# Latent attention: two heads at a time, with V as the weight and the division ahead of the transposes

## The chip, the cores and the metric

One Trainium2 chip, one of its cores. The kernel is one launch, and the metric is its device time in microseconds. Before the change three runs gave 4345.56, 4332.82 and 4324.17 us: a median of 4332.82.

## The reference, cut to what matters

The program computes two transformer blocks. The first has an RWKV mixer and then a latent attention (MLA), the second has two attentions with expert layers. The change lies in the latent attention: 16 heads, 512 queries, 768 keys (512 of the sequence and 256 of the context), 64 + 32 channels in a query or key, 64 in a value, all float32.

```python
def attend(q, k, v):
    s = jnp.einsum('bqhd,bkhd->bhqk', q, k) * (1.0 / math.sqrt(QK_NOPE + QK_ROPE))
    p = jax.nn.softmax(s, axis=-1)
    return jnp.einsum('bhqk,bkhd->bqhd', p, v)

    ...
    q = (rmsnorm(q_c, q_norm_g) @ w_qb)      # 16 heads of 64 + 32, the 32 rotated
    kv = (rmsnorm(kv_c, kv_norm_g) @ w_kvb)  # 16 heads of 64 + 64
    ...
    d_x = (o * jax.nn.silu(g_x)) @ w_out
```

## The kernel before, in words

The instructions of each engine are written out by hand, in program order, and held together by semaphores; nothing is scheduled by a tool. Data lie in one big arena (`K.arena`) and in the eight banks of PSUM (`K.ps`), 512 float32 columns each.

`MlaIn` projects the input and leaves the normed latents `QC` and `KC`, the rotated shared key `KPE` and the gate, already through silu, in `GATE` (channels on partitions). `MlaHeads` then works through 64 jobs, one for each head and block of 128 queries, four jobs of a head in a row. `Heads` holds what a job does:

- `pe_scores`: two products of 384 keys each into two banks, 0 and 1 or 2 and 3, with the query block as the weight (96x128).
- `dve_max`: VectorE takes the row maximum over 768 columns and scales it; `act_exp`: ScalarE writes the exponentials `P` and their sum.
- `pe_turn`: six 128x128 transposes of `P`, three into bank 4 and three into bank 5. VectorE copies bank 4 out (`dve_turned`, line 1550), ScalarE bank 5 (`act_turned`, line 1490), into `PT`.
- `pe_value`: six products with a piece of `PT` as the weight (128x128) and 64 columns of V, into bank 6. The queries lie on partitions there, so `dve_out` (line 1542) can divide by the sum as it copies out.

In round n TensorE issues the scores of job n, the value products of job n-2 and the transposes of job n-1:

```python
    def pe_round(self, pe, n):
        N = len(self.jobs)
        if 0 <= n < N:
            self.pe_scores(pe, n)
        if 0 <= n - 2 < N:
            self.pe_value(pe, n - 2)
        if 0 <= n - 1 < N:
            self.pe_turn(pe, n - 1)
```

Behind that each round has one piece of the projections of a head to come, given by `due(n)`: the query (3 products of 512 columns, weight 96 wide), the rope product (one), and the keys in two pieces (2 products of 384 columns each, weight 64 wide). All pieces use bank 7, so each waits until the last was copied out or used (`self.freed`). Head 0's four pieces come in rounds -5 to -2, head 1's query in round -1. V for heads 0 to 7 is made ahead of the rounds, V for heads 8 to 15 ahead of head 6's query, six groups of products one after the other, also in bank 7. POOL multiplies the query by the cosines and copies the shared key in; VectorE multiplies by the sines and adds.

`MlaOut` waits for all jobs, then transposes the output (queries on partitions) with 32 transposes into all eight banks (line 208), and VectorE gates them with eight products of 512 columns (line 1892). `FinalNorm.pe_context` comes next on TensorE: it waits for ScalarE's squares of the context (line 1927), which wait for the end of the jobs; then the output projection.

The second block's first attention, `AbHeads`, is not changed. It treats two heads at a time in the order that the change brings here: division at line 2353, copy of the turned banks at line 2321, value products at line 2283, copy of their result at line 2356.

Lines 202 and 208 are those of the helpers `mm` and `turn4`. A float32 product has two records in the trace.

Of the kernel before, what the change touches and what calls it, by code (L numbers as in the profile page):

```python
# [9 lines left out]
ALU = mybir.AluOpType  # L10
# [7 lines left out]
KT = 8  # L18
# [1387 lines left out]
class Heads:  # L1406

    def __init__(self, K, name, jobs, width, scale, value_banks):
        self.K, self.jobs, self.scale, self.value_banks = K, jobs, scale, value_banks
        s = K.s
        self.P = [K.take(T) for _ in range(4)]
        self.PT = [K.take(6, 128) for _ in range(2)]
        self.small = [K.take(8) for _ in range(12)]
        self.width = width
        self.scored, self.turned, self.valued = s[f"{name}_scored"], s[f"{name}_turned"], s[f"{name}_valued"]
        self.max, self.expd, self.sums, self.out = s[f"{name}_max"], s[f"{name}_exp"], s[f"{name}_sums"], s[f"{name}_out"]
        self.pt0, self.pt1 = s[f"{name}_pt0"], s[f"{name}_pt1"]  # L1420

        self.max_at, self.exp_at, self.sums_at = [0], [0], [0]
        for q, k, segs, masks, sink, v, kts, dst in jobs:
            copies = len(self.pieces(segs, masks)) if masks is not None else 0
            self.max_at.append(self.max_at[-1] + copies + (2 if sink is None else 3))
            self.exp_at.append(self.exp_at[-1] + (1 if sink is None else 2))
            self.sums_at.append(self.sums_at[-1] + (1 if sink is None else 2))

    @staticmethod
    def pieces(segs, masks):  # L1430

        found, o = [], 0
        for j, (a, w) in enumerate(segs):
            c = 0
            while c < w:
                d = 128
                mk = masks.get((j, c))
                while mk is None and c + d < w and (j, c + d) not in masks:
                    d += 128
                found.append((j, c, o, d, mk))  # L1440
                o += d
                c += d
        return found

    def view(self, n):

        _, _, segs, masks, _, _, _, _ = self.jobs[n]
        P, nk = self.P[n % 4], sum(w for _, w in segs)
        if masks is not None:
            return P[:, 0:nk], P[:, 0:nk], nk  # L1450
        w = segs[0][1]
        sl = 2 * (n % 2)
        return self.K.ps[:, sl:sl + len(segs), 0:w], P[:, 0:nk].rearrange("p (s n) -> p s n", n=w), nk

    def halves(self, n):
        nt = sum(w for _, w in self.jobs[n][2]) // 128
        return (0, (nt + 1) // 2), ((nt + 1) // 2, nt)

    def pe_scores(self, pe, n):
        q, k, segs, _, _, _, _, _ = self.jobs[n]  # L1460
        if n >= 2:
            pe.wait_ge(self.expd, self.exp_at[n - 1])
        for j, (a, w) in enumerate(segs):
            ins = mm(pe, self.K.ps[:, 2 * (n % 2) + j, 0:w], [(q, k[:, a:a + w])])
        ins.then_inc(self.scored, 1)

    def pe_turn(self, pe, n):
        K, P = self.K, self.P[n % 4]
        pe.wait_ge(self.expd, self.exp_at[n + 1])
        for h, (c0, c1) in enumerate(self.halves(n)):  # L1470
            if n:
                pe.wait_ge((self.pt0, self.pt1)[h], n)
            turn4(pe, K.ps[:, 4 + h, :], [P[:, c * 128:(c + 1) * 128] for c in range(c0, c1)], K.C("ident")).then_inc(self.turned, 1)

    def pe_value(self, pe, n):
        _, _, _, _, _, v, kts, dst = self.jobs[n]
        nb = len(self.value_banks)
        pe.wait_ge(self.pt0, n + 1)
        pe.wait_ge(self.pt1, n + 1)
        if n >= nb:  # L1480
            pe.wait_ge(self.out, n - nb + 1)
        mm(pe, self.K.ps[:, self.value_banks[n % nb], 0:self.width], [(self.PT[n % 2][:, c, :], v[:, kt, :]) for c, kt in enumerate(kts)]
           ).then_inc(self.valued, 1)

    def act_turned(self, act, n):
        c0, c1 = self.halves(n)[1]
        act.wait_ge(self.turned, 2 * n + 2)
        if n >= 2:
            act.wait_ge(self.valued, n - 1)
        act.activation(self.PT[n % 2][:, c0:c1, :], self.K.ps[:, 5, 0:(c1 - c0) * 128].rearrange("p (c t) -> p c t", t=128), ACT.Copy  # L1490
                       ).then_inc(self.pt1, 1)

    def act_exp(self, act, n):
        _, _, _, _, sink, _, _, _ = self.jobs[n]
        src, dst, _ = self.view(n)
        sm = self.small[n % 12]
        act.wait_ge(self.max, self.max_at[n + 1])
        if n >= 4:
            act.wait_ge(self.turned, 2 * (n - 4) + 2)
        act.activation(dst, src, ACT.Exp, bias=sm[:, 0:1], scale=self.scale, accum_out=sm[:, 1:2]).then_inc(self.expd, 1)  # L1500
        if sink is not None:
            act.activation(sm[:, 2:3], sm[:, 0:1], ACT.Exp, bias=sink).then_inc(self.expd, 1)

    def dve_max(self, dve, n):
        _, _, segs, masks, sink, _, _, _ = self.jobs[n]
        src, _, _ = self.view(n)
        mx, at = self.small[n % 12][:, 0:1], self.max_at[n]
        dve.wait_ge(self.scored, n + 1)
        if masks is not None:
            if n >= 4:  # L1510
                dve.wait_ge(self.turned, 2 * (n - 4) + 2)
            for j, c, o, d, mk in self.pieces(segs, masks):
                ps, at = self.K.ps[:, 2 * (n % 2) + j, c:c + d], at + 1
                if mk is None:
                    dve.tensor_copy(src[:, o:o + d], ps).then_inc(self.max, 1)
                else:
                    dve.tensor_tensor(src[:, o:o + d], ps, mk, ALU.add).then_inc(self.max, 1)
            dve.wait_ge(self.max, at)
        if n >= 12:
            dve.wait_ge(self.sums, self.sums_at[n - 11])  # L1520
        dve.tensor_reduce(mx, src, AX.XY if masks is None else AX.X, ALU.max).then_inc(self.max, 1)  # L1521
        dve.wait_ge(self.max, at + 1)
        if sink is None:
            dve.tensor_scalar(mx, mx, -self.scale, None, ALU.mult).then_inc(self.max, 1)
        else:
            dve.tensor_scalar(mx, mx, self.scale, sink, ALU.mult, ALU.max).then_inc(self.max, 1)
            dve.wait_ge(self.max, at + 2)
            dve.tensor_scalar(mx, mx, -1.0, None, ALU.mult).then_inc(self.max, 1)

    def dve_sums(self, dve, n):  # L1530
        sink, sm = self.jobs[n][4], self.small[n % 12]
        dve.wait_ge(self.expd, self.exp_at[n + 1])
        if sink is not None:
            dve.tensor_tensor(sm[:, 1:2], sm[:, 1:2], sm[:, 2:3], ALU.add).then_inc(self.sums, 1)
            dve.wait_ge(self.sums, self.sums_at[n] + 1)
        dve.reciprocal(sm[:, 1:2], sm[:, 1:2]).then_inc(self.sums, 1)

    def dve_out(self, dve, n):
        nb = len(self.value_banks)
        dve.wait_ge(self.valued, n + 1)  # L1540
        dve.wait_ge(self.sums, self.sums_at[n + 1])
        dve.tensor_scalar(self.jobs[n][7], self.K.ps[:, self.value_banks[n % nb], 0:self.width], self.small[n % 12][:, 1:2], None, ALU.mult
                          ).then_inc(self.out, 1)

    def dve_turned(self, dve, n):
        c0, c1 = self.halves(n)[0]
        dve.wait_ge(self.turned, 2 * n + 1)
        if n >= 2:
            dve.wait_ge(self.valued, n - 1)
        dve.tensor_copy(self.PT[n % 2][:, c0:c1, :], self.K.ps[:, 4, 0:(c1 - c0) * 128].rearrange("p (c t) -> p c t", t=128)  # L1550
                        ).then_inc(self.pt0, 1)

    def pe_round(self, pe, n):
        N = len(self.jobs)
        if 0 <= n < N:
            self.pe_scores(pe, n)
        if 0 <= n - 2 < N:
            self.pe_value(pe, n - 2)  # L1560
        if 0 <= n - 1 < N:
            self.pe_turn(pe, n - 1)

    def act_round(self, act, n):
        N = len(self.jobs)
        if 0 <= n - 1 < N:
            self.act_turned(act, n - 1)
        if 0 <= n < N:
            self.act_exp(act, n)

    def dve_round(self, dve, n):
        N = len(self.jobs)
        if 0 <= n < N:
            self.dve_max(dve, n)
# [1993 lines left out]
```

## Time and profile before

| what | us |
|---|---|
| median of three runs | 4332.82 |
| the profiled execution, its own time | 4321.39 |
| its span, first to last instruction | 4319.3 |
| latent attention, first score product to last | 316.6 |
| from there to the end of the last job | 7.5 |
| output transposes and gating, to the next product | 5.7 |

The profile is of one execution. "PE" is TensorE's products, "PEld" its weight loads, which run ahead of and beside the products; DVE is VectorE, ACT ScalarE, POOL GpSimd. An idle time is put down to the engine and line that ended it. Ends of products are modelled, and starts of loads are not.

### The profile page before, as it was taken

The page shows a single profiled execution, that of the slowest core. Times are in us where ns is not written, and L with a number is a line of the kernel's source. Part 1 is how long each engine was busy: PE and PEld are TensorE (multiplying, and loading weights), DVE is VectorE, ACT ScalarE, POOL GpSimd, SP SyncE. Part 2 cuts the span into 40 slices and gives each one's busy share as a digit, 9 for nine tenths or more (in the row PEclk, how much of TensorE's full clock was granted, in tenths as well). Part 3 has the DMA queues.
Part 4 walks back from the last instruction along what each step waited for, and adds up shares of the span by engine and source line. Part 5 has one row for each costly group of instructions (what it writes and reads, how often), then busy time and mean ns, then how long its engine had stood idle before and what let it go on. Part 6 is the DMA issues. An engine that isn't in the chain of part 4 may idle for free. (4 is left out here: it accounts for less than half of the span.)

```text
span 4319.3 us, 76089 instructions
## 1 busy us (share of the span) xinstructions
PE 3788.0 (88%) x32246; PEld 2141.1 (50%) x32246; DVE 1546.7 (36%) x3763; ACT 1353.7 (31%) x2940; POOL 197.2 (5%) x193
## 2 busy tenths in 40 slices
PE   7998687877777999998988979999969988799997
PEld 4554566666664546664565533333345454333332
DVE  3011666666673104442247231111132183211112
ACT  2002334433433123332546222222235262222222
POOL 0000000000000001000100000000012000000000
PEclk9998899999998999999999989999979999899998
DMA  5223344444443200001210249999833102699996
GB/s 207 76 84 122 93 126 120 120 115 124 118 135 99 102 22 1 20 20 38 60 46 1 101 147 386 390 390 392 329 136 92 46 1 106 252 389 386 390 394 269
DMA packets 314587, 696.04 MB, mean 161 GB/s; under 512 B 169216, under 2 KB 195968, under 8 KB 289152
## 3 DMA queue, kind: packets, MB, share of 16 engines
q1 hardware_dynamic: 293024, 612.41, 39.7%
q0 software_dynamic: 14048, 53.49, 3.6%
q10 hardware_dynamic: 7168, 25.17, 1.5%
q8 instruction: 260, 4.26, 0.4%
q14 instruction: 87, 0.71, 0.1%
HBM read 624.94 MB, written 63.71 MB: 159 GB/s over the span
## 5 line engine op out<-in xcount | busy, mean ns | idle before, releaser
L202 PE MATMUL ps<-arena 128*128 128x512 f32 (+7 forms) x5388 | 1547.7, 452 | 90.8 <-ACT arena L1137 23.9
L202 PEld LDWEIGHTS ps<-arena 128*128 128x128 f32 (+3 forms) x5388 | 889.4, 192 | 716.8 <-issue 455.8
L2693 PE MATMUL ps<-arena 128*32 128x512 f32 x9216 | 1025.7, 598 | 29.2 <-DMA arena<-in_w 24.6
L2693 PEld LDWEIGHTS ps<-arena 128*32 128x32 f32 x9216 | 307.0, 110 | 649.9 <-issue 632.9
L620 PE MATMUL ps<-arena 64*64 64x64 f32 (+1 forms) x10624 | 458.3, 240 | 176.2 <-DVE arena L1194 65.7
L620 PEld LDWEIGHTS ps<-arena 64*64 64x64 f32 x10624 | 409.5, 145 | 256.0 <-issue 105.4
L2827 DVE COPY arena<-ps 128x384 f32<-128x384 f32 x64 | 35.7, 558 | 657.1 <-PE ps L2752 657.1
L208 PE MATMUL ps<-arena 128*128 128x128 f32 x1200 | 189.9, 293 | 81.3 <-DVE arena L3146 38.0
L2803 ACT ACTIVATE arena<-ps 96x512 f32<-96x512 f32 x64 | 38.0, 593 | 624.2 <-PE ps L2693 624.2
L208 PEld LDWEIGHTS ps<-arena 128*128 128x128 f32 x1200 | 144.3, 153 | 122.7 <-DVE arena L3146 41.1
L600 DVE SCALAR_TENSOR_TENSOR arena<-arena 128x769 f32<-128x769 f32 x48 | 45.7, 1016 | 276.2 <-PE ps L202 275.9
L400 DVE SCALAR_TENSOR_TENSOR arena<-ps,arena 128x512 f32<-128x512 f32 (+1 forms) x48 | 31.8, 662 | 285.9 <-PE ps L202 285.9
L2845 DVE TENSOR_TENSOR arena<-ps,arena 64x512 f32<-64x512 f32 x64 | 43.7, 682 | 226.5 <-ACT arena L2815 226.5
L552 ACT ACTIVATE arena<-ps 128x512 f32<-128x512 f32 x64 | 30.9, 490 | 280.5 <-PE ps L202 261.5
L1521 DVE TENSOR_REDUCE arena<-ps 128x1 f32<-128x768 f32 x64 | 61.3, 958 | 158.3 <-PE ps L202 158.3
L962 PE MATMUL ps<-arena 64*64 64x64 f32 x2304 | 100.3, 243 | 16.5 <-DVE arena L1276 12.7
L2815 ACT ACTIVATE arena<-ps 64x512 f32<-64x512 f32 x64 | 38.0, 593 | 244.7 <-PE ps L2693 244.7
L344 PE MATMUL ps<-arena 128*128 128x512 f32 (+1 forms) x208 | 86.5, 581 | 20.4 <-ACT arena L335 20.4
L962 PEld LDWEIGHTS ps<-arena 64*64 64x64 f32 x2304 | 87.9, 155 | 26.7 <-DVE arena L1276 18.3
L2858 POOL DMA_INDIRECT arena<-htok,arena x64 | 57.8, 903 | 948.2 <-PE ps L2752 937.7
L253 ACT ACTIVATE arena<-arena 128x768 f32<-128x768 f32 (+1 forms) x32 | 24.5, 786 | 233.6 <-DVE arena L400 233.6
L2618 DVE TENSOR_REDUCE arena<-ps 128x1 f32<-128x768 f32 x64 | 61.0, 953 | 87.1 <-PE ps L202 87.1
(281 smaller groups left out, 3672.6 us busy)
## 6 DMA issues: line engine op xcount, KB each, us to landing
arena<-in_w SPq DMA_DIRECT2D x192, 2048.0 KB, 30.1
arena<-in_w_mod SPq DMA_DIRECT2D x24, 2048.0 KB, 8.8
arena<-in_mod_w SPq DMA_DIRECT2D x12, 2048.0 KB, 9.0
yb<-arena ACTq DMA_DIRECT2D x64, 384.0 KB, 10.0
arena<-in_rwkv_w_in SPq DMA_DIRECT2D x8, 2048.0 KB, 9.9
arena<-rkvg SPq DMA_DIRECT2D x38, 384.0 KB, 4.0
rkvg<-arena POOLq DMA_DIRECT2D x32, 384.0 KB, 3.0
arena<-di SPq DMA_DIRECT2D x192, 64.0 KB, 2.5
```

The costliest lines, as they stand in the source:

```text
L202: ins = pe.matmul(out, l, r, start=(i == 0), stop=(i == len(pairs) - 1))
L208: ins = pe.transpose(bank[:, i * 128:(i + 1) * 128], src, ident)
L344: ins = pe.matmul(out, w[:, k, :], self.H[:, k, a:a + n], start=(k == 0), stop=(k == KT - 1), skip_group_check=True)
L600: dve.scalar_tensor_tensor(self.LPs[j % 2][:, k, 1:n + 1], self.XX[:, k, 1:n + 1], self.K.PR("mu")[:, 8 * j + k:8 * j + k + 1], self.H[:, ...
L620: ins = pe.matmul(out[p, :], l[p, :], r[p, :], start=(i == 0), stop=(i == len(pairs) - 1))
L962: ins = pe.matmul(out[p, :], src[p, :], ident[p, p], start=True, stop=True)
L1521: dve.tensor_reduce(mx, src, AX.XY if masks is None else AX.X, ALU.max).then_inc(self.max, 1)
L2618: dve.tensor_reduce(sm[:, c:c + 1], self.scores_at(n, c), AX.XY, ALU.max).then_inc(self.max, 1)
L2693: return pe.matmul(bank[32 * at:32 * at + 32, :], left[:, k, 32 * g:32 * g + 32], right[:, k, :], start=first, stop=last)
L2803: act.activation(self.moe.AC[i % 2][0:ROWS, :], A[0:ROWS, :], ACT.Silu).then_inc(self.silu, 1)
L2845: dve.tensor_tensor(YS[0:64, 512:1024], ps[0:64, 7, :], YS[0:64, 512:1024], ALU.add).then_inc(self.y1, 1)
L2858: pool.indirect_dma_start(out=moe.HG[i % 3][0:ROWS, :], out_offset=None, in_=self.K.scr["htok"][0:moe.nt, :], in_offset=bass.IndirectOffse ...
```

## The change

Jobs are taken for two heads at a time: jobs 8i to 8i+7 alternate between heads 2i and 2i+1. Q, K and their pieces have four buffers each in place of two, and both heads of a pair must be ready before its first job, so pieces start at round -9. VectorE takes the reciprocal of the sum and multiplies `P` by it ahead of the transposes, which come three jobs late; one ScalarE copy empties both banks. The value products of two jobs come together in odd rounds, with V as the weight (64 wide), one head into partitions 0 to 63 of bank 6 and the other into 64 to 127. Channels lie on partitions then, so the copy out of the bank also gates, and `MlaOut`'s transposes and gating go.

```diff
-class Heads:
...
 class MlaHeads:
...
+    FIRST, LAST = -9, 68
...
-        self.VV, self.OT = K.take(6, D), K.take(4, D)
-        self.Qs, self.Ks = [K.take(TX) for _ in range(2)], [K.take(T) for _ in range(2)]
+        self.VV, self.O = K.take(6, D), K.take(KT, TX)
+        self.Qs, self.Ks = [K.take(TX) for _ in range(4)], [K.take(T) for _ in range(4)]
...
-        h, part = divmod(n + 5, 4)
+        h, part = divmod(n + 9, 4)
         return (h, part) if 0 <= h < 16 else None
+    @staticmethod
+    def job(n):
+        return 2 * (n // 8) + n % 2, n % 8 // 2
...
+    def pe_turn(self, pe, n):
+        pe.wait_ge(self.normed, n + 1)
+        if n:
+            pe.wait_ge(self.pt, n)
+        for b in range(2):
+            ins = turn4(pe, self.K.ps[:, 4 + b, :], [self.P[n % 4][:, i * 128:(i + 1) * 128] for i in range(3 * b, 3 * b + 3)], self.K.C("ident"))
+        ins.then_inc(self.turned, 1)
+
+    def pe_value(self, pe, p):
+        pe.wait_ge(self.pt, 2 * p + 2)
+        if p:
+            pe.wait_ge(self.out, p)
+        for t in range(6):
+            for c in range(2):
+                h, _ = self.job(2 * p + c)
+                ins = pe.matmul(self.K.ps[64 * c:64 * c + 64, 6, 0:128], self.VV[:, t, 64 * h:64 * h + 64], self.PT[c][:, t, :], start=(t == 0),
+                                stop=(t == 5), skip_group_check=True)
+        ins.then_inc(self.valued, 1)
...
-        for n in range(-5, 66):
...
-            self.heads.pe_round(pe, n)
+        for n in range(self.FIRST, self.LAST):
+            if 0 <= n < self.N:
+                if n % 8 == 0:
+                    h = n // 4 + 1
...
+                self.pe_scores(pe, n)
+            if n >= 5 and n % 2:
+                self.pe_value(pe, (n - 5) // 2)
+            if 0 <= n - 3 < self.N:
+                self.pe_turn(pe, n - 3)
             if due := self.due(n):
...
+            j = n - 3
+            if 0 <= j < self.N:
+                act.wait_ge(self.turned, j + 1)
+                if j >= 2:
+                    act.wait_ge(self.valued, j // 2)
+                act.activation(self.PT[j % 2].rearrange("p (b i) t -> p b (i t)", b=2), ps[:, 4:6, 0:384], ACT.Copy).then_inc(self.pt, 1)
+            if 0 <= n < self.N:
+                sm = self.small[n % 8]
+                act.wait_ge(self.max, 2 * n + 2)
...
+                act.activation(self.P[n % 4].rearrange("p (s n) -> p s n", s=2), self.scores(n), ACT.Exp, bias=sm[:, 0:1], scale=self.SCALE,
+                               accum_out=sm[:, 1:2]).then_inc(self.expd, 1)
...
+            j = n - 1
+            if 0 <= j < self.N:
+                sm, P = self.small[j % 8], self.P[j % 4]
+                dve.wait_ge(self.expd, j + 1)
+                dve.reciprocal(sm[:, 2:3], sm[:, 1:2]).then_inc(self.sums, 1)
+                dve.wait_ge(self.sums, j + 1)
+                dve.tensor_scalar(P, P, sm[:, 2:3], None, ALU.mult).then_inc(self.normed, 1)
+            if n >= 5 and n % 2:
+                p = (n - 5) // 2
+                h, qb = self.job(2 * p)
+                at = self.O[:, h // 2, 128 * qb:128 * qb + 128]
+                dve.wait_ge(self.valued, p + 1)
+                dve.tensor_tensor(at, ps[:, 6, 0:128], self.into.GATE[:, h // 2, 128 * qb:128 * qb + 128], ALU.mult).then_inc(self.out, 1)
...
 class MlaOut:
...
         self.heads.over(pe)
-        for i in range(8):
-            qb, c = divmod(i, 2)
-            turn4(pe, K.ps[:, i, :], [self.heads.OT[:, qb, m * 128:(m + 1) * 128] for m in range(4 * c, 4 * c + 4)], K.C("ident")
-                  ).then_inc(s["mla_chan"], 1)
-        pe.wait_ge(s["mla_gated"], 8)
         fin.pe_context(pe)
         self.proj.pe(pe, fin)
```

How it moves TensorE's instructions. In the steady loop, from one head's query piece on, before (L202 128x64 x6 are the value products, 128x384 x2 the scores, 64x384 x2 a key piece, 96x512 x3 the query, 96x512 the rope product, L208 the transposes):

```order
L202 MATMUL ps<-arena 96x512 x3
L202 MATMUL ps<-arena 128x384 x2
L202 MATMUL ps<-arena 128x64 x6
L208 MATMUL ps<-arena 128x128 x6
L202 MATMUL ps<-arena 96x512
L202 MATMUL ps<-arena 128x384 x2
L202 MATMUL ps<-arena 128x64 x6
L208 MATMUL ps<-arena 128x128 x6
L202 MATMUL ps<-arena 64x384 x2
```

and with the change (L1633 are the new value products):

```order
L202 MATMUL ps<-arena 96x512 x3
L202 MATMUL ps<-arena 128x384 x2
L208 MATMUL ps<-arena 128x128 x6
L202 MATMUL ps<-arena 96x512
L202 MATMUL ps<-arena 128x384 x2
L1633 MATMUL ps<-arena 64x128 x12
L208 MATMUL ps<-arena 128x128 x6
L202 MATMUL ps<-arena 64x384 x2
```

Every second round has no value products, and the others have twelve, of 128 columns.

At the end of the stage, before:

```order
L208 MATMUL ps<-arena 128x128 x6
L202 MATMUL ps<-arena 128x64 x6
L208 MATMUL ps<-arena 128x128 x6
L202 MATMUL ps<-arena 128x64 x6
L208 MATMUL ps<-arena 128x128 x32
L202 MATMUL ps<-arena 128x256 x8
```

and with the change, from the last scores on:

```order
L202 MATMUL ps<-arena 128x384 x2
L1633 MATMUL ps<-arena 64x128 x12
L208 MATMUL ps<-arena 128x128 x12
L1633 MATMUL ps<-arena 64x128 x12
L208 MATMUL ps<-arena 128x128 x12
L1633 MATMUL ps<-arena 64x128 x12
L202 MATMUL ps<-arena 128x256 x8
```

The 32 transposes are gone, and four turns and three pairs of value products now follow the last scores, where two turns and three jobs' value products did.

VectorE in one round with a rope product, before:

```order
L1521 TENSOR_REDUCE arena<-ps 128x1
L1524 TENSOR_SCALAR arena<-arena 128x1
L1536 RECIPROCAL arena<-arena 128x1
L1542 TENSOR_SCALAR arena<-ps,arena 128x64
L1550 COPY arena<-ps 128x384
L1842 TENSOR_TENSOR arena<-ps,arena 96x512
```

and with the change:

```order
L1724 TENSOR_REDUCE arena<-ps 128x1
L1726 TENSOR_SCALAR arena<-arena 128x1
L1731 RECIPROCAL arena<-arena 128x1
L1733 TENSOR_SCALAR arena<-arena 128x768
L1747 TENSOR_TENSOR arena<-ps,arena 96x512
```

The division over 768 columns takes the place of the copy of 384 and of the division on the way out; the gated copy (line 1739) stands in odd rounds only.

## Rows read from the trace of the kernel before

**Rows 1.** The page, part 1: busy us, share of the span, instructions.
```profile
PE 3788.0 (88%) x32246; PEld 2141.1 (50%) x32246; DVE 1546.7 (36%) x3763; ACT 1353.7 (31%) x2940; POOL 197.2 (5%) x193
```
**Rows 2.** Windows: the loop and the drain; us, busy by engine, clock, DMA.
```profile
1632.90:1949.50 316.60, 312.37 (x1620) 206.51 (x1619) 145.18 (x341) 113.93 (x239) 31.23 (x30) 1.00 0.04 14
1949.50:1957.00 7.50, 5.92 (x49) 5.26 (x47) 3.31 (x9) 2.24 (x6) 0.00 (x0) 1.00 0.01 3
```
**Rows 3.** Waits in 1632.9 to 1949.5: total us, times, longest.
```profile
ACT arena L1490 <- PE ps L208: 170.4, 62, 3.0
DVE arena L1521 <- PE ps L202: 157.3, 63, 19.6
```
**Rows 4.** Timeline, weight loads, rounds without a piece: start us, us, what.
```profile
1941.06 0.70 PEld L208 LDWEIGHTS ps<-arena 128*128 128x128 f32 x6
1941.72 2.71 PEld L202 LDWEIGHTS ps<-arena 96*128 96x128 f32 x16
1944.30 0.69 PEld L208 LDWEIGHTS ps<-arena 128*128 128x128 f32 x6
```
**Rows 5.** Timeline, weight loads: value products of the last job but one, alone.
```profile
1952.31 1.42 PEld L202 LDWEIGHTS ps<-arena 128*128 128x128 f32 x12 [0.83 <-DVE arena L1550]
1953.59 0.70 PEld L208 LDWEIGHTS ps<-arena 128*128 128x128 f32 x6
```
**Rows 6.** Timeline, transposes' loads over one head's four rounds.
```profile
1747.10 0.70 PEld L208 LDWEIGHTS ps<-arena 128*128 128x128 f32 x6
1751.19 0.70 PEld L208 LDWEIGHTS ps<-arena 128*128 128x128 f32 x6
...
1766.75 0.70 PEld L208 LDWEIGHTS ps<-arena 128*128 128x128 f32 x6
```
**Rows 7.** Timeline of the second block's first attention.
```profile
2350.41 0.64 PEld L208 LDWEIGHTS ps<-arena 128*128 128x128 f32 x6 [0.17 <-issue]
2351.33 0.81 ACT L2321 ACTIVATE arena<-ps 128x768 f32<-128x768 f32 x1 [0.55 <-PE ps L208]
2352.25 0.64 PEld L208 LDWEIGHTS ps<-arena 128*128 128x128 f32 x6 [0.73 <-DVE arena L2353]
2353.05 1.29 PEld L2283 LDWEIGHTS ps<-arena 128*64 128x64 f32 x24 [0.17 <-issue]
...
2354.51 0.64 PEld L208 LDWEIGHTS ps<-arena 128*128 128x128 f32 x6 [0.17 <-issue]
```
**Rows 8.** Timeline, TensorE: head 0's query piece, and head 1's, its first.
```profile
1621.03 2.79 PE L202 MATMUL ps<-arena 128*96 128x512 f32 x6 [0.78 <-ACT arena L1810]
...
1630.62 6.26 PE L202 MATMUL ps<-arena 128*96 128x512 f32 x16 [0.57 <-ACT arena L1830]
```
**Rows 9.** Groups in 2217 to 2415: busy us, mean ns, idle before.
```profile
L2336 DVE TENSOR_REDUCE arena<-ps 128x1 f32<-128x768 f32 x32 | 30.5, 953 | 12.0 <-PE ps L2253 12.0
L2353 DVE TENSOR_SCALAR arena<-arena 128x768 f32<-128x768 f32 x32 | 18.4, 618 | 0.6
L2356 DVE COPY arena<-ps 128x128 f32<-128x128 f32 x47 | 13.5, 287 | 30.4 <-PE ps L2283 29.9
...
L2321 ACT ACTIVATE arena<-ps 128x768 f32<-128x768 f32 x47 | 38.1, 811 | 29.5 <-PE ps L208 29.5
L2311 ACT ACTIVATE arena<-ps,arena 128x768 f32<-128x768 f32 x32 | 28.7, 900 | 3.7 <-DVE arena L2339 3.1
L2311 ACT ACTIVATION_READ_ACCUMULATOR arena<-ps,arena 128x1 f32 x88 | 17.7, 201 | 0.0
```
**Rows 10.** Timeline: the last job's copy, the context's squares, the context's product.
```profile
1956.71 0.28 DVE L1542 TENSOR_SCALAR arena<-ps,arena 128x64 f32<-128x64 f32 x1 [1.92 <-PE ps L202]
1957.03 1.91 ACT L1927 ACTIVATE arena<-arena 128x2048 f32<-128x2048 f32 x1 [1.98 <-DVE arena L1542]
...
1962.68 0.70 PE L202 MATMUL ps<-arena 128*128 128x256 f32 x2 [1.91 <-DVE arena L1892]
```
**Rows 11.** Waits in 2217 to 2415: total us, times, longest.
```profile
PEld ps L208 <- DVE arena L2353: 22.4, 25, 1.3
```

More of the change, by code:

```diff
@@ L1405, in over @@
         e.wait_ge(self.proj.added, self.proj.total)
-class Heads:
[L1411 to L1574, printed above, removed]
-        if 0 <= n - 1 < N:
-            self.dve_sums(dve, n - 1)
-        if 0 <= n - 2 < N:
-            self.dve_out(dve, n - 2)
-        if 0 <= n - 1 < N:
-            self.dve_turned(dve, n - 1)
-    def over(self, e):
-        N = len(self.jobs)
-        e.wait_ge(self.out, N)
-        e.wait_ge(self.pt1, N)
-        e.wait_ge(self.sums, self.sums_at[N])
@@ L1599, in __init__ @@
         self.sq, self.rk, self.kw = K.take(5, T), K.take(T), K.take(SLOT)
+        self.end = K.top
         self.sums = Sums(K, "mlan", [self.sq[:, k, :] for k in range(2)], self.rstd, T)
@@ L1732, in __init__ @@
         K.top = into.inner
-        self.VV, self.OT = K.take(6, D), K.take(4, D)
-        self.Qs, self.Ks = [K.take(TX) for _ in range(2)], [K.take(T) for _ in range(2)]
+        self.VV, self.O = K.take(6, D), K.take(KT, TX)
+        self.Qs, self.Ks = [K.take(TX) for _ in range(4)], [K.take(T) for _ in range(4)]
         self.rt = K.take(TX)
-        jobs = []
-        for h in range(16):
-            for qb in range(4):
-                jobs.append((self.Qs[h % 2][0:96, qb * 128:(qb + 1) * 128], self.Ks[h % 2][0:96, :], SEGS, None, None,
-                             self.VV[:, :, 64 * h:64 * h + 64], range(6), self.OT[:, qb, 64 * h:64 * h + 64]))
-        self.heads = Heads(K, "mla", jobs, 64, 1.0 / math.sqrt(96), (6,))
+        self.P = [K.take(T) for _ in range(4)]
+        K.top = max(K.top, into.end)
+        self.PT = [K.take(6, 128) for _ in range(2)]
+        self.small = [K.take(4) for _ in range(8)]
         s = K.s
         self.mm, self.evac = s["mlah_mm"], s["mlah_evac"]
-        self.O = None
+        self.scored, self.turned, self.valued = s["mlah_scored"], s["mlah_turned"], s["mlah_valued"]
+        self.max, self.expd, self.sums, self.normed = s["mlah_max"], s["mlah_exp"], s["mlah_sums"], s["mlah_normed"]
+        self.pt, self.out = s["mlah_pt"], s["mlah_out"]
     def mm_at(self, h, what):
@@ L1755, in due, with scores @@
     def due(n):
-        h, part = divmod(n + 5, 4)
+        h, part = divmod(n + 9, 4)
         return (h, part) if 0 <= h < 16 else None
+    @staticmethod
+    def job(n):
+        return 2 * (n // 8) + n % 2, n % 8 // 2
+    def scores(self, n):
+        return self.K.ps[:, 2 * (n % 2):2 * (n % 2) + 2, 0:384]
     def over(self, e):
-        self.heads.over(e)
+        e.wait_ge(self.out, self.N // 2)
     def pe_values(self, pe, c):
@@ L1834, in dve @@
         self.into.over(dve)
-        for n in range(-5, 66):
-            self.heads.dve_round(dve, n)
+        for n in range(self.FIRST, self.LAST):
+            if 0 <= n < self.N:
+                mx = self.small[n % 8][:, 0:1]
+                dve.wait_ge(self.scored, n + 1)
+                if n >= 8:
+                    dve.wait_ge(self.normed, n - 7)
+                dve.tensor_reduce(mx, self.scores(n), AX.XY, ALU.max).then_inc(self.max, 1)
+                dve.wait_ge(self.max, 2 * n + 1)
+                dve.tensor_scalar(mx, mx, -self.SCALE, None, ALU.mult).then_inc(self.max, 1)
+            j = n - 1
[11 more added lines that the diff above has]
+                dve.tensor_tensor(at, ps[:, 6, 0:128], self.into.GATE[:, h // 2, 128 * qb:128 * qb + 128], ALU.mult).then_inc(self.out, 1)
             if due := self.due(n):
                 h, part = due
-                Q = self.Qs[h % 2][0:96, :]
+                Q = self.Qs[h % 4][0:96, :]
                 if part == 1:
                     dve.wait_ge(self.mm, self.mm_at(h, "rope"))
+                    if h:
+                        dve.wait_ge(s["mlah_rope"], 2 * h)
                     dve.tensor_tensor(self.rt[0:96, :], ps[0:96, 7, :], K.C("mS")[0:96, 0:TX], ALU.mult).then_inc(s["mlah_rope"], 1)
@@ L1867, in __init__ @@
         self.K, self.s, self.into, self.heads = K, K.s, into, heads
-        self.O = K.take(KT, TX)
-        self.proj = OutProj(K, "mla", K.I["mla_w_out"], [self.O[:, k, :] for k in range(KT)], K.MODS[1], 16, ((0, 0, TX),),
+        self.proj = OutProj(K, "mla", K.I["mla_w_out"], [heads.O[:, k, :] for k in range(KT)], K.MODS[1], 16, ((0, 0, TX),),
                             ((heads.mm, heads.mm_at(7, "q")), (heads.mm, heads.mm_at(15, "q"))), first=3)
```

46 lines of the change are left out of this document (23 added, 23 removed).

## The prediction, made before the changed kernel was run

> **What bounds the kernel now.** I read the page first: on one core TensorE is busy for 88% of the span [rows 1], more than twice any other engine. The change touches one stage only, the latent attention, so everything after is read there. The windows [rows 2] show it from the first score matmul at 1632.9 us to the last at 1949.5: 316.6 us, TensorE busy 312.4, VectorE 145.2, ScalarE 113.9, and the granted clock 1.00, the full 2.4 GHz. The waits [rows 3] say who waits: ScalarE (170.4 us before its copies) and VectorE (157.3 us before its maxima) both wait for TensorE. So the loop is worth what its TensorE instructions issue, and I price it from the starts of weight loads, which unlike modelled matmul ends are events: a group costs the time to the next group's first load.
>
> **TensorE's round today.** Without a projection piece one round (six transposes, two scores, six value products) takes 1944.30 - 1941.06 = 3.24 us, of which the transposes take 1941.72 - 1941.06 = 0.66 [rows 4]. Six value products alone take 1953.59 - 1952.31 = 1.28 [rows 5]. That leaves 1.30 for the scores. A head's four rounds take 1766.75 - 1747.10 = 19.65 us [rows 6], so the four projection pieces issue for 19.65 - 4 x 3.24 = 6.69 us a head; the rope piece alone for 1751.19 - 1747.10 - 3.24 = 0.85.
>
> **1. The value products.** Each job's six products with a 128x128 weight (the turned exponentials) and 64 columns become, for two jobs, twelve with a 128x64 weight (V) and 128 columns, alternately into the lower and the upper half of the bank. This form runs already in the next attention, at line 2283: 24 records (two to a float32 product) take 2354.51 - 2353.05 = 1.46 us, with 0.17 us of nothing behind the last load, and the transposes ahead of them take 0.80 in place of 0.66 [rows 7]. I take a pair at 1.46 + 0.80 - 0.66 = 1.60 us against 2 x 1.28 = 2.56 now: 0.96 saved, times 32 pairs: **-30.7 us**. The bounds: 24 records at half of a 64-column product's issue (1.28/12/2 = 0.053 us) without any gap give 1.28 and -41.0; the two halves not overlapping give 24 x 0.107 + 0.31 = 2.9 and +11. I take the row of the same shape, the nearest there is. By the first sentence alone the term would be the -41.0; the gaps in rows 7 agree with the second, and this kernel pays them twice a pair.
>
> **2. Two heads before the first score.** The rounds now begin at -9 and not -5: head 1's four pieces run bare behind head 0's, where before three lay in rounds 0 to 2. Bare, each waits for the copy of the one before, since all share bank 7: head 0 took 1630.62 - 1621.03 = 9.6 us [rows 8] for 6.7 of issue. **+2.9 us**.
>
> **3. The loop's other waits.** Transposes come three jobs late, so a job's chain (maximum, exponential, division) has two more rounds. Only one pair of banks receives transposes, as before, but now one ScalarE copy of 768 columns empties both (0.81 us) in place of a 384 copy on each of two engines. From a turn's first load through its copy to the next dependent load takes 2352.25 - 2350.41 = 1.84 us [rows 7], so 1.18 us after the turn's issue is over. Between a turn and the next product or turn that needs its copy TensorE has the next scores, 1.30, and the piece: 1.30 + 0.85 = 2.15 or more while pieces last. It fits everywhere, by 0.1 us where there are none. ScalarE's exponential (0.90 and an accumulator read of 0.20) stands behind the copy in its queue. In the last nine rounds, which have no piece (before it was five), an odd job's exponential ends some 0.15 us after the scores that reuse its banks could start: four times, **+0.6 us**. VectorE has per job 0.95 for the maximum, 0.62 for the division over 768 columns and 0.29/2 for the gated copy (priced as the copy of line 2356), 1.7 us, and its one-column instructions and rope work as now; ScalarE 0.81 + 0.90 + 0.20 = 1.9 us and its copies of pieces as now [rows 9]. TensorE's mean round becomes (19.65 - 2 x 0.96)/4 = 4.43. So the division and the larger copy I cost at nothing: TensorE's issue hides them. If that cover went, they would cost 0.62 + 0.81 us a job, 92 us. The V set for heads 8 to 15 moves four rounds ahead and costs what it did. POOL's two instructions a head run a full round before they are needed. SP's second load of output weights starts four rounds sooner and was not waited for.
>
> **4. The drain.** After the last scores TensorE still issues four turns and three value pairs, 4 x 0.66 + 3 x 1.60 = 7.4 us, with four waits of 1.18 us for a copy (turn 61, pair 60-61, turn 63, pair 62-63) and some 0.6 us to the end of the last gated copy: 12.7. Before it was the 7.5 us window [rows 2], for 2 x 0.66 + 3 x 1.28 = 5.2 us of issue. The extra idle time is (12.7 - 7.4) - (7.5 - 5.2) = **+3.0 us**.
>
> **5. The end.** The 32 transposes of the output and the eight gating products go. From the end of the last copy, 1956.71 + 0.28, to the next product at 1962.68 was 5.7 us [rows 10]. The next product is the context's sum, which needs ScalarE's squares: 1.91 us, started when heads are over, hidden so far under the gating. It is late next: 1.91 + 0.15 stay. **-3.6 us**.
>
> **Sum.** -30.7 + 2.9 + 0.6 + 3.0 - 3.6 = -27.8 us. Against the profiled execution's own 4321.4 us: 4293.6. That execution lies 11.4 us below the median of the three runs, 4332.8; set against the median, as the result will be, it is **4305 us**, 0.64% less. Nothing downstream has a fixed date: the loads of the next part start on semaphores of this one and move with it.
>
> **Rivals.** *The pair does not overlap* (here V, not turned exponentials, is the weight for both, and the two moving operands differ): 2.9 us a pair, so +11 in place of -30.7, and with the other terms +14 us: 4347, within 0.5%. Rows 7 speak against it: there, too, the two halves have different moving operands. Chance 0.04.
>
> *TensorE waits at every turn* (the slower side). This order of work, run in the next attention, does leave TensorE waiting: 22.4 us in 25 waits for the division at line 2353 [rows 11]. The place is the turn: it waits for the job's division and for the copy of the turn before. If each of 64 turns waited a further 1 us, +64 gives +36 us: 4369. Today's time is crossed at 27.8/64 = 0.43 us a turn, and ahead of that the margins must go: 0.1 us in rounds without a piece, 2.15 - 1.18 = 1.0 with the shortest piece. Against it: there the rounds have no projection pieces to fill the time, here 55 of 64 have. A rule of the Trainium skill feeds this one (SBUF — State Buffer, its part on the port pair that VectorE and GpSimd share): a VectorE tensor_scalar over SBUF can hold or wait for that pair for a whole instruction. By it a division could stand behind one of POOL's two instructions a head; no row here has both at once. Chance 0.07.
>
> *The gain is mostly eaten by small stalls*: 0.2 us a round, as where a queue's order bites, gives 13 us back: -15, 4318, within 0.5%. For it: margins of 0.1 us in the tail, and two more switches of tile shape beside scores than rows 7 can show. Chance 0.19.
>
> *The change does nothing at all* cannot be: the order of instructions shows the twelves and no 32 transposes.
>
> **How the numbers follow.** The forecast (-28, give or take 6) has 0.70. About 0.5%, 21.7 us, is what a measurement of this kernel can tell from no change; the forecast lies just past it, so a tenth of its chance falls short of that by the scatter of a median (the three runs span 21 us), and a little comes back from the small-stall case. Faster 0.66, within 0.5% 0.27, slower 0.07. Range: down to the gap-free pair and scatter, -41 + 3 - 9, 4286; up to the small-stall case with scatter of 8, 4326. What is left out is the slower case, the part without overlap, and bad luck.
>
> **What would show it.** Right: 24 records of the new value line in about 1.3 us of loads; even rounds with rope of 2.8 us and a cycle of four rounds of 17.7; head 1 bare before the first score, which comes 9.6 us later after the first projection; 12.7 us from last score to last gated copy; then 2.1 to the context's product; clock 1.00. Wrong: TensorE waiting for the division or the copy inside the loop for over 10 us in all, a pair of more than 2 us, or a granted clock under 1.00 in the stage.

## The result, and the profile after

The changed kernel took 4304.05 us, the median of five runs (4298.65 to 4305.8), against 4332.82 us, the median of five runs of the kernel before (4324.17 to 4345.56): a ratio of 0.9935, 95% interval 0.9921 to 0.9948. The forecast was 4305 us.

TensorE's share on the page is nearly what it was in [rows 1], with 29 us less of busy time:

```profile
PE 3759.1 (87%) x32214; PEld 2095.4 (49%) x32214; DVE 1533.8 (36%) x3723; ACT 1372.6 (32%) x2940; POOL 201.0 (5%) x193
```

The profiled execution's span is 4300.9 us, only 18.4 less than before, though the medians differ by 28.8. The stage has to be looked at by itself. These are TensorE's rows from its first V group on (start us, us, what, idle time before and what ended it), in the trace of the kernel before and then of the changed one:

```profile
1604.83 1.98 PE L202 MATMUL ps<-arena 128*128 128x512 f32 x4 [0.69 <-ACT arena L1685]
```

```profile
1613.91 1.98 PE L202 MATMUL ps<-arena 128*128 128x512 f32 x4 [0.69 <-ACT arena L1505]
...
1630.11 2.79 PE L202 MATMUL ps<-arena 128*96 128x512 f32 x6 [0.78 <-ACT arena L1681]
...
1639.71 2.81 PE L202 MATMUL ps<-arena 128*96 128x512 f32 x6 [0.57 <-ACT arena L1713]
...
1649.25 12.10 PE L202 MATMUL ps<-arena 128*96 128x512 f32 x32 [0.57 <-ACT arena L1713]
...
1943.68 11.85 PE L202 MATMUL ps<-arena 128*128 128x256 f32 x35 [2.42 <-ACT arena L1818]
```

The stage began 9.1 us later in this execution, ahead of anything that the change touches. From the first V group to the context's product it took 1962.68 - 1604.83 = 357.85 us before and 1943.68 - 1613.91 = 329.77 us now: **-28.1 us**. I call this the stage's time below; it moves far less between executions than the span does. From that product to the end it was 2356.6 us before and 2357.2 now.

The loop, TensorE's weight loads over four rounds, which answer to [rows 6]:

```profile
1677.37 1.29 PEld L1633 LDWEIGHTS ps<-arena 128*64 128x64 f32 x24 [0.55 <-issue]
1678.83 0.64 PEld L208 LDWEIGHTS ps<-arena 128*128 128x128 f32 x6 [0.17 <-issue]
...
1695.08 1.29 PEld L1633 LDWEIGHTS ps<-arena 128*64 128x64 f32 x24 [0.55 <-issue]
1696.54 0.64 PEld L208 LDWEIGHTS ps<-arena 128*128 128x128 f32 x6 [0.17 <-issue]
```

Four rounds take 1696.54 - 1678.83 = 17.71 us in place of 19.65: 0.97 us less for each pair. The new value products issue for 1.46 us, as they do in [rows 7].

The drain, in which TensorE, VectorE and ScalarE take turns:

```profile
1928.28 1.53 PE L1633 MATMUL ps<-arena 128*64 128x128 f32 x24
1929.74 0.87 PE L208 MATMUL ps<-arena 128*128 128x128 f32 x6
1931.61 0.85 PE L208 MATMUL ps<-arena 128*128 128x128 f32 x6 [0.99 <-ACT arena L1693]
1933.35 1.53 PE L1633 MATMUL ps<-arena 128*64 128x128 f32 x24 [0.90 <-ACT arena L1693]
1934.82 0.87 PE L208 MATMUL ps<-arena 128*128 128x128 f32 x6
1936.68 0.85 PE L208 MATMUL ps<-arena 128*128 128x128 f32 x6 [0.99 <-ACT arena L1693]
1938.43 2.83 PE L1633 MATMUL ps<-arena 128*64 128x128 f32 x24 [0.90 <-ACT arena L1693]
```

```profile
1941.30 0.29 DVE L1739 TENSOR_TENSOR arena<-ps,arena 128x128 f32<-128x128 f32 x1 [6.08 <-PE ps L1633]
```

```profile
1941.62 1.91 ACT L1818 ACTIVATE arena<-arena 128x2048 f32<-128x2048 f32 x1 [3.25 <-DVE arena L1739]
```

All four waits for ScalarE's copy (line 1693) are there, and the last pair takes 2.83 us and not 1.53. The windows answer to [rows 2] and tell why. The third last number of a row is the granted clock, as a fraction of 2.4 GHz:

```profile
1651.40:1928.10 276.70, 272.58 (x1556) 155.82 (x1554) 135.16 (x307) 127.38 (x234) 31.37 (x28) 1.00 0.05 16
1928.10:1938.40 10.30, 6.54 (x73) 5.13 (x72) 3.18 (x9) 4.72 (x8) 0.00 (x0) 1.00 0.00 0
1938.40:1941.50 3.10, 2.83 (x24) 2.43 (x24) 0.20 (x1) 0.00 (x0) 0.00 (x0) 0.51 0.00 0
...
1943.60:1948.00 4.40, 4.32 (x18) 3.53 (x19) 0.00 (x0) 0.00 (x0) 0.00 (x0) 1.00 0.02 4
```

The last pair ran at 0.51, about 1.2 GHz, behind a drain with four waits. Before, a stretch of low clock came one step later, behind the gating, on the context's product:

```profile
1962.60:1967.00 4.40, 4.32 (x12) 3.53 (x13) 0.02 (x1) 0.00 (x0) 0.00 (x0) 0.61 0.00 0
```

### The profile page after: what moved, and what is told of

The parts are those of the page before. It is cut to its first block and busy times, and to the rows that moved or that the text cites. A ratio compares the mean times of both kernels' runs of the same rounds, so it can differ in the third digit from the quotient of the medians.

```text
span 4300.9 us, 75825 instructions
## 1 busy us (share of the span) xinstructions
PE 3759.1 (87%) x32214; PEld 2095.4 (49%) x32214; DVE 1533.8 (36%) x3723; ACT 1372.6 (32%) x2940; POOL 201.0 (5%) x193
## 5 line engine op out<-in xcount | busy, mean ns | idle before, releaser
L202 PE MATMUL ps<-arena 128*128 128x512 f32 (+8 forms) x4620 | 1458.6, 479 | 95.6 <-ACT arena L1137 23.9
L202 PEld LDWEIGHTS ps<-arena 128*128 128x128 f32 (+5 forms) x4620 | 786.5, 190 | 707.1 <-issue 457.4
L2584 PE MATMUL ps<-arena 128*32 128x512 f32 x9216 | 1022.6, 596 | 31.1 <-DMA arena<-in_w 26.5
L620 PEld LDWEIGHTS ps<-arena 64*64 64x64 f32 x10624 | 415.3, 146 | 255.2 <-issue 103.5
L208 PE MATMUL ps<-arena 128*128 128x128 f32 x1168 | 189.0, 296 | 83.6 <-DVE arena L3037 41.4
L208 PEld LDWEIGHTS ps<-arena 128*128 128x128 f32 x1168 | 140.3, 150 | 140.2 <-DVE arena L3037 44.9
L1724 DVE TENSOR_REDUCE arena<-ps 128x1 f32<-128x768 f32 x64 | 61.3, 958 | 142.3 <-PE ps L202 142.3
L962 PEld LDWEIGHTS ps<-arena 64*64 64x64 f32 x2304 | 92.0, 161 | 25.8 <-DVE arena L1276 17.8
L216 PE MATMUL ps<-arena 128*32 128x512 f32 x576 | 75.5, 646 | 19.6 <-DMA arena<-in_w_mod 15.5
```

Of the source, the lines that this page charges most:

```text
L202: ins = pe.matmul(out, l, r, start=(i == 0), stop=(i == len(pairs) - 1))
L208: ins = pe.transpose(bank[:, i * 128:(i + 1) * 128], src, ident)
L216: ins = pe.matmul(out[32 * j:32 * j + 32, :], cs[:, 4 * half + j, :], w[:, 4 * half + j, :], start=(half == 0), stop=(half == 1))
L620: ins = pe.matmul(out[p, :], l[p, :], r[p, :], start=(i == 0), stop=(i == len(pairs) - 1))
L962: ins = pe.matmul(out[p, :], src[p, :], ident[p, p], start=True, stop=True)
L1724: dve.tensor_reduce(mx, self.scores(n), AX.XY, ALU.max).then_inc(self.max, 1)
```

## The experiments

All are variants of the changed kernel; all times are medians, and "the stage's time" is from the profiled execution, first V group to the context's product. Each variant was profiled once, and the changed kernel was not run beside the later ones, so they are compared with it by the stage's time. That time needs one correction. Three microseconds or so of low clock fall on the last pair in the changed kernel, inside the stage; in other variants they fall on the context's product, just behind it, or do not come. These are the last pair and that product with the halves apart, with two jobs late, and with more banks:

```profile
1971.87 2.46 PE L1633 MATMUL ps<-arena 128*64 128x128 f32 x24 [0.90 <-ACT arena L1693]
1976.74 19.11 PE L202 MATMUL ps<-arena 128*128 128x256 f32 x48 [2.41 <-ACT arena L1818]
```

```profile
1933.13 1.53 PE L1633 MATMUL ps<-arena 128*64 128x128 f32 x24 [0.90 <-ACT arena L1693]
1937.08 19.11 PE L202 MATMUL ps<-arena 128*128 128x256 f32 x48 [2.43 <-ACT arena L1818]
```

```profile
1913.20 1.53 PE L1642 MATMUL ps<-arena 128*64 128x128 f32 x24 [0.90 <-ACT arena L1706]
1917.15 17.43 PE L202 MATMUL ps<-arena 128*128 128x256 f32 x48 [2.43 <-ACT arena L1831]
```

In the changed kernel the same two took 2.83 and 17.43; with the halves apart 2.46 is what every pair takes. A pair at full clock is worth 1.3 us of the stage's time; the product at low clock costs 1.7 us behind the stage, where that time does not see it.

The changed kernel run again beside the first three variants:

> The changed kernel again, as the yardstick on this chip for the runs beside it: 28 us under the kernel before, 0.6 to 0.7%.

It took 4304.97 us against 4332.79 for the kernel before: ratio 0.994, interval 0.9924 to 0.9957. The stage's time was 329.76 us, within 0.01 of the other execution's, although the stage began at 1609.23 and not at 1613.91 us.

**Are the two halves worth it, or the narrow weight?**

```diff
-        for t in range(6):
-            for c in range(2):
+        for c in range(2):
+            for t in range(6):
                 h, _ = self.job(2 * p + c)
```

> The same twelve value products of a pair, but all six of one head first, then all six of the other, so that neighbours go to the same half of the columns. Theory (the two halves run side by side, and that is the gain): a pair costs 24 records at 0.107 us and 0.3 for the switches, 2.9 us in place of 1.6; 32 pairs give +41 us over the changed kernel, some 13 us over the kernel before. Rival (the gain is the narrow weight, or the moving of 128 columns per load): the pair stays at 1.6 us and the time that of the changed kernel.

4335.19 us, ratio 1.000 (0.9989 to 1.0011) to the kernel before, 30.2 us over the changed one run beside it; stage's time 358.02, 28.3 more. The value products' loads and what follows them:

```profile
1683.11 2.21 PEld L1633 LDWEIGHTS ps<-arena 128*64 128x64 f32 x24 [0.55 <-issue]
1685.49 0.64 PEld L208 LDWEIGHTS ps<-arena 128*128 128x128 f32 x6 [0.17 <-issue]
```

A pair issues for 1685.49 - 1683.11 = 2.38 us and not 1.46: 0.92 us for each of 32 pairs is 29.4 us. The stage shows 28.3 because its last pair ran at full clock, 1.3 us less; with the 1.7 us behind the stage it comes to 30.0, against 30.2 by the medians. So the gain of the change hangs on the alternation between the two halves; V as a narrow weight without it keeps 0.04 of the 0.96 us a pair. The rival is refuted. My price for this case was too high all the same: a record takes 2.38/24 = 0.099 us, gaps included, not the 0.107 that I had taken from products with a weight 128 wide.

**Is the division hidden?** A second instruction behind it:

```diff
-                dve.tensor_scalar(P, P, sm[:, 2:3], None, ALU.mult).then_inc(self.normed, 1)
+                dve.tensor_scalar(P, P, sm[:, 2:3], None, ALU.mult).then_inc(s["mlah_extra"], 1)
+                dve.wait_ge(s["mlah_extra"], j + 1)
+                dve.tensor_scalar(P, P, 1.0, None, ALU.mult).then_inc(self.normed, 1)
```

> A second VectorE instruction over the 768 exponentials (times 1.0) behind the division, 64 times 0.62 us = 40 us of added VectorE work ahead of the transposes. Theory (VectorE is hidden with two rounds to spare): +0 to 2 us over the changed kernel, all of it in the last nine rounds, and TensorE waits for the division in less than 2 us. Rival (the chain through the division is exposed in part): +10 to +40 us.

4306.13 us, 1.2 over the changed kernel; stage's time 329.74, the same to 0.02 us, with 48.2 us more of work on VectorE. The groups (busy us, mean ns, idle before):

```profile
L1724 DVE TENSOR_REDUCE arena<-ps 128x1 f32<-128x768 f32 x64 | 61.0, 953 | 95.1 <-PE ps L202 95.1
L1735 DVE TENSOR_SCALAR arena<-arena 128x768 f32<-128x768 f32 x64 | 48.2, 753 | 2.2
```

VectorE's wait for scores shrank from 142.3 to 95.1 us, by the work that was added: it is cover, and the division, itself 39.7 us of VectorE's work, costs no time that the stage shows. To see where the cover ends, three added instructions:

> Three further VectorE instructions over the 768 exponentials behind the division. The second cost VectorE 0.75 us a job and the clock nothing; three cost 2.3 us a job, so VectorE has 1.7 + 0.3 + 0.3 + 2.3 = 4.7 us of work a job against 4.4 us that TensorE issues. Theory (the cover is TensorE's issue, and it ends there): VectorE becomes the bound, +0.3 us for each of 55 jobs with a piece and 4.3 - 2.8 = 1.5 us for the nine without, some +30 us over the changed kernel. Rival (the chain of one job counts, not the sum: two rounds of 4.4 us hide 2.3 us more): +0 to 5 us in the rounds with pieces, under +15 in all.

4323.48 us against 4327.41 for the kernel before beside it, ratio 0.9995 (0.9984 to 1.0006): some 24 us over the changed kernel by the ratios, stage's time 349.29, 19.5 more. That is between the theory (30) and its rival (under 15). Two of TensorE's rows show what neither had:

```profile
1904.74 2.99 PE L202 MATMUL ps<-arena 128*64 128x384 f32 x8 [0.72 <-DVE arena L1753]
...
1922.07 1.56 PE L202 MATMUL ps<-arena 96*128 96x384 f32 x4 [0.94 <-ACT arena L1699]
```

With pieces, TensorE waits not for the division but for VectorE's rope product, which is queued behind it and holds bank 7: 9.8 us in 13 waits up to 1905 us. From 1655 to 1905 us VectorE was busy for 212 of 250 us, some 4.2 us for each of 51 jobs and not 4.7, so it was not the bound there. In rounds without pieces it nearly was (39 of the next 41 us): the exponentials come late, because VectorE's maxima do, and the waits from there to the end of the drain make most of the other half of the 19.5 us. The context's product took 20.37 us, 2.9 more than in the changed kernel, at low clock, which takes the 19.5 to 22.4 of the 24. The cover is 0.75 us a job at least and less than 2.3.

**Do the transposes have to be three jobs late?** Two variants move them, and the value products with them (here for one job late):

```diff
-            if n >= 5 and n % 2:
-                self.pe_value(pe, (n - 5) // 2)
-            if 0 <= n - 3 < self.N:
-                self.pe_turn(pe, n - 3)
+            if n >= 3 and n % 2 == 1:
+                self.pe_value(pe, (n - 3) // 2)
+            if 0 <= n - 1 < self.N:
+                self.pe_turn(pe, n - 1)
```

> Transposes one job late and not three, value products one round behind. Theory: the division of job n-1 stands on VectorE behind the maximum of job n, which waits for its scores, so it ends 2.3 us after them; TensorE waits that long in rounds without value products and 0.7 us in the others: 3.0 us a pair, 96 us in all, less 2 us in the drain: some +94 us over the changed kernel, and the wait named is that for the division's line. Rival (lateness is not needed, the copy decides): under +10 us.

4432.22 us, 127.3 over the changed kernel, ratio 1.0229 (1.0207 to 1.025) to the kernel before; stage's time 453.99, 124.2 more. The waits of the loads and of the products (total us, times, longest) and two of the transposes' loads:

```profile
PEld ps L208 <- DVE arena L1733: 104.7, 62, 2.6
PE ps L208 <- DVE arena L1733: 77.8, 62, 2.0
```

```profile
1802.23 0.64 PEld L208 LDWEIGHTS ps<-arena 128*128 128x128 f32 x6 [2.58 <-DVE arena L1733]
...
1808.92 0.64 PEld L208 LDWEIGHTS ps<-arena 128*128 128x128 f32 x6 [0.74 <-DVE arena L1733]
```

The mechanism is as forecast, long waits where there are no value products and short ones where there are. The size is not, and the windows say why. The clock was granted at 0.90 over these 405 us; the second and third rows are the whole stage, first V group to the context's product, one job late and in the changed kernel:

```profile
1655.00:2060.00 405.00, 323.06 (x1593) 172.68 (x1592) 136.66 (x308) 129.87 (x236) 29.16 (x28) 0.90 0.03 11
1618.42:2072.41 453.99, 356.47 (x1712) 186.00 (x1713) 142.58 (x320) 141.58 (x254) 34.37 (x32) 0.91 0.03 10
1609.23:1938.99 329.76, 309.82 (x1712) 172.53 (x1713) 141.37 (x320) 140.56 (x254) 36.58 (x32) 0.99 0.04 14
```

TensorE's same 1712 records were busy for 46.7 us more and TensorE was idle for 77.6 us more, 124.2 in all. So the waits came to less than the forecast's 94 us, and the rest is slower products. The clock gives that rest its size: a tenth below full speed on average is a fifth of the time, 81 us, at 1.2 GHz, and if TensorE was busy through all of it that costs 40 us. What is left is near the error of the split, since ends of products are modelled and one that a wait follows counts as busy to its end. I read it that waits of this length cost a second time, through the clock; no run holds the clock and keeps the waits, so that the waits bring the clock down is not shown.

> Transposes two jobs late, value products in even rounds. Theory (two is enough: the division ends 2.3 us after the next scores, and TensorE needs it 2.8 us or more after them; the drain is one round shorter): -1 us against the changed kernel, no wait for the division in the loop. Rival (three are needed): waits for the division of about 0.5 us a round, +30 us.

4300.04 us, ratio 0.9939 (0.9919 to 0.996) to the kernel before, which took 4331.42 in this set of runs; stage's time 327.20, 2.6 less than the changed kernel's. No wait for the division is listed in the loop. So two jobs late is enough, and the rival is refuted. Of the 2.6 us, 1.3 is the last pair at full clock, and it is no gain: the low clock moved to the context's product and cost 1.7 us there. The other 1.3 is the drain that is a round shorter. With both moves of the clock 0.9 us is left, the forecast's 1, and too little for the medians to tell.

**What the bare stretches cost.** Both sets of V and the pieces of heads 0 and 1 spread over the free banks:

```diff
+    @staticmethod
+    def piece_bank(h, part):
+        return 7 - part if h < 2 else 7
...
-            pe.wait_ge(*self.freed)
-            mm(pe, self.K.ps[:, 7, :], [(self.into.KC[:, k, tt * 128:(tt + 1) * 128], kw[:, k, 8 * c:8 * c + 8, 64:128]) for k in range(2)]
+            b = 7 - tt if c == 0 else 7 - tt % 2
+            if c == 1 and tt == 1:
+                self.freed[b] = self.out, self.v_after
+            pe.wait_ge(*self.freed[b])
+            mm(pe, self.K.ps[:, b, :], [(self.into.KC[:, k, tt * 128:(tt + 1) * 128], kw[:, k, 8 * c:8 * c + 8, 64:128]) for k in range(2)]
...
```

> The changed kernel with both sets of V and the pieces of heads 0 and 1 spread over several banks in place of bank 7 alone, so that only the rope product waits for a copy. Theory (these stretches pay a bare copy per group): 10 gaps of 0.95 us between the V groups, 0.9 twice behind them, and 2.0 us for each of two heads: -15 us against the changed kernel, half before the first scores. Rival (the copies on ScalarE set the pace, or the gaps hide nothing): under 4 us.

4282.63 us, ratio 0.9891 (0.9874 to 0.9907); stage's time 312.27, 17.5 less than the changed kernel's. TensorE ahead of the first scores:

```profile
1604.88 13.14 PE L202 MATMUL ps<-arena 128*128 128x512 f32 x30 [0.69 <-ACT arena L1505]
1618.70 6.57 PE L202 MATMUL ps<-arena 96*96 96x512 f32 x16 [0.68 <-ACT arena L1722]
1625.95 15.85 PE L202 MATMUL ps<-arena 96*96 96x512 f32 x42 [0.68 <-ACT arena L1722]
```

Three waits are left, two of them for the query's own copy. From the first V group to the first transposes it takes 36.8 us in place of 47.3, 10.5 less, of which 4.7 lie from head 0's rope product on, in the pieces of heads 0 and 1; that is more than the 2.9 us of waiting that the change had added there. The second V set, 1714.96 to 1734.83 up to the next transposes in the changed kernel, takes 5.7 us less. Together these are 16.2 us for the 15 forecast; the other 1.3 of the 17.5 is the last pair at full clock.

**What the context's product waits for.** The squares also move in the arena, to where the weights of keys and values were, since their own place overlaps buffers of the heads:

```diff
+            if n == 64:
+                act.activation(self.CQ, self.K.X[:, :, TX:T], ACT.Square).then_inc(self.s["fin_ctx"], 1)
...
-        act.activation(self.CQ, K.X[:, :, TX:T], ACT.Square).then_inc(s["fin_ctx"], 1)
```

> The changed kernel with ScalarE's squares of the context moved from behind the heads into the drain, behind the copy of job 61. Theory (with the gating gone these squares are what the context's product waits for): the 2.1 us between the last gated copy and the product fall to 0.1 to 0.2, -1.9 us, to be read in the trace, since the timing cannot tell it. Rival (the product waits for something else): no change of that gap.

4300.33 us, ratio 0.9933 (0.9916 to 0.9949); the timing cannot tell it, as said, but the trace can. The last gated copy, and the product's loads:

```profile
1943.88 0.29 DVE L1742 TENSOR_TENSOR arena<-ps,arena 128x128 f32<-128x128 f32 x1 [6.08 <-PE ps L1634]
1944.22 3.84 PEld L202 LDWEIGHTS ps<-arena 128*128 128x128 f32 x18 [0.80 <-DVE arena L1742]
```

The gap fell from 2.1 us to 0.05, and the stage's time to 327.74, by 2.0.

**All three together.**

> Two late, more banks and early squares together: the sum of the three, -18 us against the changed kernel, -46 us or 1.07% against the kernel before. Rival: they overlap and give less than 12 together.

4280.0 us, ratio 0.9891 (0.9873 to 0.9909), the same as the banks alone; stage's time 310.11, 19.7 less than the changed kernel's, where the parts add up to 22.1. Nearly all of the missing 2.4 is the clock's. Two jobs late and the banks each contain 1.3 us for a last pair at full clock; the three together can win it once at most, and here the pair took 2.53 us, so they won 0.3. That is 2.3 of the 2.4, and a turn that waits 1.14 us in place of 0.99, behind the squares in ScalarE's queue, makes up the rest. So the parts add up, the forecast was 18, and the rival is refuted for the stage. Against the kernel before it is 51 us, and some 24 more than the changed kernel's 28, but the timing cannot tell it from the banks alone.

## Why the prediction was right

That the median came within 1 us of the forecast's 4305 is luck, with runs that span 7 and 21 us. The stage's 28.1 us against the forecast's 27.8 is the better test, and its steps can be told one by one:

- **Value products, -30.7 forecast.** 28 pairs, in the rounds with pieces and behind the last scores, at 0.97, and four in the rounds without pieces at 2 x 3.24 - (1917.06 - 1911.46) = 0.88 (loads of line 1633 at these times): -30.7, with what the tail lost (4 x 0.09 = 0.4) already in it. The row of the same shape in another stage was the right price. The gap-free bound of -41 was never near: the 0.17 us behind the pair's last load stand here as in [rows 7]. The trace agrees with the Trainium skill (TensorEngine Tiling (Array Packing), Tiling Modes), by which a change of mode drains the engine.
- **Two heads first, +2.9.** Head 1 took 1649.25 - 1639.71 = 9.5 us bare for 6.7 of issue: +2.9.
- **Other waits, +0.6.** 0.4, counted above. Inside the loop TensorE is not listed as waiting for the division, and for the turned copy only 1.6 us in three waits, none longer than the 0.55 us that lie ahead of a pair's loads anyway; VectorE waits for scores 142.3 us and ScalarE for transposes 123.4, where it was 157.3 and 170.4 in [rows 3].
- **Drain, +3.0.** From the end of the last scores' issue (1928.1) to the end of the last gated copy (1941.59) it took 13.5 us and not 12.7, and +3.8 of idle and slow time. The four waits are as forecast; the step that was mis-sized is the last pair, 1.1 us longer in its loads (2.43 against 1.29) at half clock. I had taken the clock as 1.00 throughout and named less than that in the stage as a sign of being wrong. That sign came up, for 3 of 330 us; it did not touch the loop, on which the sum rests.
- **End, -3.6.** 1943.68 - 1941.59 = 2.1 us in place of 5.7: -3.6. With +3.8 for the drain these make -27.6 of the 28.1.

With the low clock gone from the context's product and the projection's first part (17.43 us for the same 48 records against 19.14) 1.7 us came back just behind the stage, for the 1.3 lost on the last pair. Neither move was forecast, and that they nearly cancel is luck.

Of the rivals, the pair that does not overlap would have given 0 and not +14 us against the kernel before, as the run with the halves apart shows: I had priced the pair at 2.9 us, and it took some 2.5. Waiting at every turn is what one job late does, and it costs more than its waits. The margin was there, since one job less (two late) still fits and two less does not; the 0.1 us that I gave it in rounds without a piece no run measures. The rule on the port pair that VectorE and GpSimd share (the Trainium skill, SBUF — State Buffer, Who interferes with whom) can now be seen. The division's and POOL's rows in the changed kernel:

```profile
1684.87 0.62 DVE L1733 TENSOR_SCALAR arena<-arena 128x768 f32<-128x768 f32 x1
1685.18 1.44 POOL L1763 TENSOR_TENSOR arena<-arena 96x512 f32<-96x512 f32 x1 [15.39 <-PE ps L202]
```

POOL's product took 1.44 us where it met the division, against 1.26 before, and a round of slack hid it. With two jobs late the two do not meet, and all 16 took 1.26 to 1.28 us with VectorE's rope product still beside them, so it is the division that they met. The second instruction of the doubled division met it the other way round, behind POOL's, 1.51 us at worst against 0.56 (least, median and longest in ns):

```profile
L1735 DVE TENSOR_SCALAR arena<-arena x64: 559/560/1510, 1654.9 to 1930.7; 128x768 f32<-128x768 f32 x64
```

The trace agrees with the rule that one of the two waits. It did not reach TensorE: the stage's time was the same.

## What to carry to other kernels

Where one engine issues without a gap, price a change by the starts of its instructions, from a stage that already runs the same shapes, and add the stretches ahead of the loop and behind it, where every wait is bare: here they took back some 7 us of 34, and stretches of that kind gave 16 when they were mended. An engine that is not the bound can take a third more work for nothing (48 us on 141 here), but only if the order of its queue leaves the bound's next need ahead of it. Compare stages and not spans where the scatter upstream is half the effect, and look just behind the stage's end before you book a microsecond: a stretch of low clock can have moved across it.

## What was not expected of the hardware

- Products of a 64-wide weight with 128 columns take 2.38 us for 24 records when neighbours use the same half of the columns, and 1.46 when they alternate; a 128-wide weight with 64 columns took 2.56 for as many.
- Behind a drain with four waits of 0.9 to 1.0 us the clock fell to about half for some 3 us on the last pair (changed), a step later on the next product (halves apart, and two late behind three waits), and with more banks, whose drain is the same to 0.01 us, not at all. So the drain alone does not decide it, and what does is open. In a loop whose loads waited 0.7 and 2.6 us in turn it was granted at 0.90 on average. In the other loops it was 1.00, also with four instructions at the division, where 13 waits made 9.8 us.
- The start of the stage lay between 1604.8 and 1618.7 us over eleven profiled executions with the same instructions ahead of it, a spread of half the effect that was measured, and between 1609.2 and 1618.7 in four that ran on the same chip. The changed stage itself, profiled twice, repeated to 0.01 us.
